# Six layer norms: the shift moves from GpSimd to VectorE

## What is computed

```python
def _ln(x, g, b):
    xf = x.astype(jnp.float32)
    mu = jnp.mean(xf, axis=-1, keepdims=True)
    var = jnp.mean(jnp.square(xf - mu), axis=-1, keepdims=True)
    return ((xf - mu) * lax.rsqrt(var + LN_EPS) * g.astype(jnp.float32) + b.astype(jnp.float32)).astype(x.dtype)

def _post(x, sub, g, b):
    return _ln(ALPHA * x + sub, g, b)
...
        yp = _post(yp, mix_p, ln_mix_g[i], ln_mix_b[i])
...
        yp = _post(yp, _cross_attn(yp, mk, mv, w_xq[i], w_xo[i]), ln_x_g[i], ln_x_b[i])
...
        yp = _post(yp, _swiglu(yp, w_gate[i], w_up[i], w_down[i]), ln_ff_g[i], ln_ff_b[i])
```

## Time and profile before

| | before |
|---|---|
| time, median of 3 runs | 3909.61 us (3906.79 to 3910.99) |
| the profiled execution: its time | 3911.87 us |
| the profiled execution: its span | 3910.1 us |
| mean granted TensorE clock | 0.942 |
| busy: PE, DVE, ACT, POOL | 3417.1, 1464.8, 1002.7, 536.6 us |
| chain that ended last: PE, DVE, ACT, POOL | 74%, 11%, 3%, 2% |

### The profile page before, as it was taken

The page is one execution under the profiler, slowest core; times in us unless marked ns, Lnnn a source line. Parts: engine busy times, 40 slices in busy tenths (PEclk is TensorE's granted clock), DMA queues, the critical chain, the costliest instruction groups (busy, mean ns, idle before and its releaser), DMA issues.

```text
span 3910.1 us, 54622 instructions
## 1 busy us (share of the span) xinstructions
PE 3417.1 (87%) x21246; PEld 3193.1 (82%) x21246; DVE 1464.8 (37%) x2121; ACT 1002.7 (26%) x1311; POOL 536.6 (14%) x331
## 2 busy tenths in 40 slices
PE   7985779799889999999599965687999799999996
PEld 6973458797889999999589954686978699999996
DVE  1555443424342212113404367755143522122125
ACT  2123442423231011012323323434232311111112
POOL 1663101200120000001300032012001300000003
PEclk9987999999999999999899988899999899999997
DMA  4673741324111111111121114322251111111111
GB/s 131 208 230 111 232 141 49 118 100 153 43 32 43 43 49 43 46 46 38 41 81 54 59 57 143 111 64 76 80 207 47 33 43 43 48 48 44 43 36 56
DMA packets 366672, 319.80 MB, mean 82 GB/s; under 512 B 19616, under 2 KB 308817, under 8 KB 366147
## 3 DMA queue, kind: packets, MB, share of 16 engines
q1 hardware_dynamic: 354783, 299.86, 24.8%
q10 hardware_dynamic: 11620, 17.77, 1.3%
q0 software_dynamic: 144, 0.52, 0.0%
HBM read 287.69 MB, written 30.74 MB: 81 GB/s over the span
## 4 chain that ended last, share of the span: by engine, by line
PE 74%; DVE 11%; DMA 5%; issue 5%; ACT 3%; POOL 2%; SPq 1%; DVEq 0%; ACTq 0%; POOLq 0%
PE ps L319 63%; PE ps L1649 2%; PE ps L1671 1%; DVE spl_w L304 1%; POOL kpage L1100 1%; PE ps L977 1%; DVE acc L2266 1%; DVE x L1444 1%; PE ps L705 1%; DMA acc<-spill_d 1%; DMA raw_w<-in_w_xv 1%; PE ps L1627 1%; DMA vpage<-in_cache_fox_v 1%; PE ps L1027 1%; ACT x L1458 1%
## 5 line engine op out<-in xcount | busy, mean ns | idle before, releaser
L319 PE MATMUL ps<-xs,spl_w 128*128 128x344 f32 x12528 | 2010.7, 323 | 55.5 <-DVE spl_w L304 27.5
L319 PEld LDWEIGHTS ps<-xs,spl_w 128*128 128x128 f32 x12528 | 2003.4, 191 | 60.1 <-DVE spl_w L304 29.5
L304 DVE TENSOR_TENSOR spl_w<-raw_w,spl_w 128x1024 fp32r<-128x1024 f32 x268 | 334.2, 1247 | 765.6 <-ACT spl_w L300 760.9
L319 PE MATMUL ps<-hs,spl_w 128*128 128x344 f32 x3168 | 513.8, 325 | 27.5 <-DVE hs L1862 27.5
L319 PEld LDWEIGHTS ps<-hs,spl_w 128*128 128x128 f32 x3168 | 512.2, 193 | 29.0 <-issue 29.0
L300 ACT CAST spl_w<-raw_w 128x1024 fp32r<-128x1024 f32 x268 | 279.5, 1043 | 393.7 <-PE ps L319 364.9
L1398 POOL MEMSET sum_x<- 128x1032 f32 x6 | 5.9, 984 | 1604.9 <-DVE hs L1862 1376.4
L1860 DVE TENSOR_TENSOR sum_x<-sq,ps 128x1032 f32<-128x1032 f32 x44 | 54.1, 1229 | 351.4 <-PE ps L319 351.4
L1406 POOL TENSOR_TENSOR sum_x<-sum_x,x 128x1032 f32<-128x1032 f32 x48 | 116.1, 2418 | 471.9 <-DVE x L1366 187.5
L1100 POOL TENSOR_TENSOR kpage<-kpage,qb 128x1024 f32<-128x1024 f32 x64 | 154.9, 2447 | 104.7 <-DMA kpage<-in_cache_fox_k 104.4
L1844 ACT CAST hs<-sum_x 128x1032 f32 (+1 forms) x44 | 46.4, 1056 | 472.2 <-DVE sum_x L1860 472.2
(11 more groups left out here) (358 smaller groups left out, 2909.0 us busy)
## 6 DMA issues: line engine op xcount, KB each, us to landing
kpage<-in_cache_fox_k SPq DMA_DIRECT2D x128, 256.0 KB, 3.2
vpage<-in_cache_fox_v SPq DMA_DIRECT2D x128, 256.0 KB, 3.0
raw_w<-in_w_gate SPq DMA_DIRECT2D x44, 512.0 KB, 3.7
raw_w<-in_w_up SPq DMA_DIRECT2D x44, 512.0 KB, 3.7
mkv<-in_cache_mem_k SPq DMA_DIRECT2D x16, 1024.0 KB, 7.9
mkv<-in_cache_mem_v SPq DMA_DIRECT2D x16, 1024.0 KB, 5.0
raw_w<-in_w_down SPq DMA_DIRECT2D x32, 512.0 KB, 3.9
raw_w<-in_w_in_cd SPq DMA_DIRECT2D x28, 512.0 KB, 3.6
```

The lines of the kernel that those rows point to most:

```text
L304: dve.tensor_tensor(spl_w[:, s, 1], raw_w[:, s], spl_w[:, s, 0].bitcast(F32), ALU.subtract).then_inc(lo_ready, 1)
L319: mm = pe.matmul(ps[:, 3 * s + t, 0:width], spl_w[:, s, a, k], part[:, k, width * t:width * (t + 1)], start=(k == 0 and step == 0), stop=( ...
```

## The change

DVE does the shift too. In the loop of norms 1, 2 and 4 it now does, per round, the product of chunk k+2, the shift of chunk k+1 and the low part of chunk k; the shift of chunk 0 stands ahead of the loop and that of chunk 7 behind it. In norms 0 and 3 each shift follows the product of the same chunk at once. In norm 5 the order per chunk is product, shift, copies. POOL's three loops of shifts are gone; its sums and everything else stay. Names, semaphores and arithmetic are the same.

```diff
--- before.py
+++ after.py
@@ -1443,11 +1443,11 @@
             xk = chunk(x, k)
             dve.tensor_tensor(xk, xk, sum_sq[:], ALU.mult).then_inc(sem("ln_scaled"), 1)
 
-        def pool_norm_shift(pool, ln, k):
-            pool.wait_ge(sem("ln_dve_step"), 2 * ln + 2)
-            pool.wait_ge(sem("ln_scaled"), DC * ln + k + 1)
+        def dve_norm_shift(dve, ln, k):
+            dve.wait_ge(sem("ln_dve_step"), 2 * ln + 2)
+            dve.wait_ge(sem("ln_scaled"), DC * ln + k + 1)
             xk = chunk(x, k)
-            pool.tensor_tensor(xk, xk, sum_x[:], ALU.add).then_inc(sem("ln_shifted"), 1)
+            dve.tensor_tensor(xk, xk, sum_x[:], ALU.add).then_inc(sem("ln_shifted"), 1)
 
         def act_norm_affine(act, ln, k):
             g = cols[:, ds(LN_G[ln] + k, 1)]
@@ -1554,6 +1554,7 @@
         def dve_memory(dve, L, ln):
             g0 = G0[f"mem{L}"]
             dve_norm_scale(dve, ln, 0)
+            dve_norm_shift(dve, ln, 0)
             for q in range(2):
                 def body(i, last=False):
                     g = g0 + 4 * q + i
@@ -1561,6 +1562,7 @@
                     split_lo(dve, 0, g + 1)
                     if not last:
                         dve_norm_scale(dve, ln, 4 * q + i + 1)
+                        dve_norm_shift(dve, ln, 4 * q + i + 1)
                     for s in range(2):
                         m = 16 * L + 8 * q + 2 * i + s
                         dve.wait_ge(sem("mem_rowsT"), m + 3)
@@ -1573,8 +1575,6 @@
                     loop(dve, 3, body)
                     body(3, last=True)
 
-        def pool_memory(pool, L, ln):
-            loop(pool, DC, lambda i: pool_norm_shift(pool, ln, i))
 
 
 
@@ -1792,19 +1792,20 @@
             act_norm_stats(act, ln)
             loop(act, DC, lambda k: act_norm_affine(act, ln, k))
 
-        def pool_norm(pool, ln):
-            loop(pool, DC, lambda k: pool_norm_shift(pool, ln, k))
 
         def dve_norm(dve, ln):
             split_lo(dve, 1, next_pair(ln))
             dve_norm_stats(dve, ln)
             dve_norm_scale(dve, ln, 0)
             dve_norm_scale(dve, ln, 1)
+            dve_norm_shift(dve, ln, 0)
 
             def body(k):
                 dve_norm_scale(dve, ln, k + 2)
+                dve_norm_shift(dve, ln, k + 1)
                 dve_norm_lo(dve, ln, k)
             loop(dve, DC - 2, body)
+            dve_norm_shift(dve, ln, DC - 1)
             dve_norm_lo(dve, ln, DC - 2)
             dve_norm_lo(dve, ln, DC - 1)
 
@@ -1891,9 +1892,12 @@
             dve_norm_stats(dve, LAST)
             dve_norm_scale(dve, LAST, 0)
             dve_norm_scale(dve, LAST, 1)
+            dve_norm_shift(dve, LAST, 0)
             for c in range(DC):
                 if c + 2 < DC:
                     dve_norm_scale(dve, LAST, c + 2)
+                if c + 1 < DC:
+                    dve_norm_shift(dve, LAST, c + 1)
                 dve.wait_ge(sem("xT_ready"), len(tiles) + c + 1)
                 if c >= 2:
                     dve.wait_ge(sem(f"rows_stored{c % 2}"), 16 * (NT // 2 + 2 * (c // 2)))
@@ -2571,12 +2575,9 @@
                     pool_states(pool)
                     pool_heads(pool)
                 pool_sums(pool, ("ab_out", "cd_out_y")[L], 3 * L)
-                pool_memory(pool, L, 3 * L)
                 pool_cross(pool, L)
                 pool_sums(pool, f"xo{L}", 3 * L + 1)
-                pool_norm(pool, 3 * L + 1)
                 pool_sums(pool, f"down{L}_2", 3 * L + 2)
-                pool_norm(pool, 3 * L + 2)
 
         @block.tensor
         def _(pe):
```

## The result

| | before | with the change |
|---|---|---|
| time, first comparison | 3908.2 us (median of 4) | 3881.15 us (3878.54 to 3882.97, 4 runs) |
| ratio, 95% interval | | 0.993 [0.9915, 0.9946] |
| ratio, two later comparisons | | 0.9937 [0.9925, 0.9949] and 0.9932 [0.9918, 0.9945] |
| the profiled execution's span | 3910.1 us | 3881.0 us |
| busy: PE, DVE, ACT, POOL | 3417.1, 1464.8, 1002.7, 536.6 us | 3412.7, 1465.8, 1002.3, 399.6 us |

A forecast was written before the change was run, and what follows sets the result against it. TensorE holds 74% of the chain; in norms 1, 2 and 4 it waits while VectorE's and GpSimd's instructions run in turn. Terms of 14.0 + 7.5 + 0.7 + 0.9 = 23.1 us gave 3888.8 or 3886.5, stated as 3888; range 3881 to 3898.

The forecast's parts named there:

- norm 1, TensorE going on: Norm 1's loop: rounds of 3.45 us instead of 4.49, TensorE's end at 35.0 instead of 42.0, 7.0 us gained.
- norm 4: Norm 4's loop, same pattern of rows as norm 1: 7.0 us gained.
- norm 2: Norm 2's tail: the next weights' load moves with the last low part, 30.10 instead of 37.59, 7.5 us gained.
- last norm: Last norm: copies keep their pace, only the start gets shorter; 0.7 us, taken between 0 and 2.0.
- norms 0 and 3, TensorE going on: Memory rounds: shifts fit into idle time, and GpSimd's stretching of a first-round low part ends; 0.9 us for both.
- The first chunk ran at the low clock: TensorE's first chunk in norms 1 and 4: about 4.8 us near 1.2 GHz; a second slow chunk would cost 1.3 us a norm.
- the 2.8 us between runs: Range's lower end, 3881: 2.8 us taken off the sum on the median for scatter between runs.
- 2.7 for handoffs: Range's lower end, 3881: a further 2.7 us taken off for handoffs shorter between some instructions.
- the memory rounds give it back: Rival, norms 0 and 3: shifts in VectorE's in-order queue hold TensorE, costing 17.5 us and the 0.9; 3906, chance 0.06.
- the slow product is VectorE's own: Rival, norms 1, 2 and 4: the loop, not GpSimd, makes the product 3.42 us; about 3970 and slower, chance 0.03.
- ScalarE did not set the pace: Rival, norms 1, 2 and 4: ScalarE's way over 4.60 us makes the pace 4.0 us; 8 us less gain, 3896, chance 0.08.
- The rule of the Trainium skill: VectorE's loop rounds: three full durations, 3.69 us; some 3.6 us less gain over three norms, about 3892.

The follow-up runs named there:

- e5: The changed kernel, with GpSimd also adding two SBUF tiles into a spare one, once per chunk in norms 1 and 4; 3909.01 us in one run.
- e4: The kernel before, with the shift moved to VectorE only in norms 0, 3 and 5; ratio 1.000 [0.9989, 1.0011].
- e7: The changed kernel plus one unused VectorE maximum, about 2.2 us, in each of the seven memory rounds with a shift; 3889.74 us in one run.

## Why the prediction came out as it did

**The mechanism was right, and the terms too.** Each of them, as forecast and as the profiles have it:

| term | forecast | measured |
|---|---|---|
| norm 1, TensorE going on (43.96 to 36.78) | 7.0 us | 7.2 us |
| norm 4 (44.0 to 36.77) | 7.0 us | 7.2 us |
| norm 2 (57.29 to 49.38) | 7.5 us | 7.9 us |
| last norm (38.31 to 37.79, 37.41, 38.10) | 0.7 us | 0.5 us (0.2 to 0.9) |
| norms 0 and 3, TensorE going on (mean 76.17 to 75.75, twice) | 0.9 us | 0.8 us |
| sum | 23.1 us | 23.6 us |

The steps inside held as well: the first low part at 7.57 (7.58), chunk 5's at 24.82 (24.74), the last at 30.10 (29.79), TensorE's end at 35.0 (34.8), the last copy at 32.5 (32.56). The last low part came 0.3 us earlier than forecast: 0.2 of it since it started 0.04 us after ScalarE's second instruction (1094.76 to 1094.80), not 0.26, and 0.1 since that instruction ended sooner. The first chunk ran at the low clock as forecast, and part of the second too. TensorE had no matmul for 13.89 us up to 1073.97; the windows from there on (PE, PEld, DVE, ACT, POOL busy, then the granted clock):

```profile
1073.90:1078.30 4.40, 4.33 (x15) 4.36 (x16) 4.40 (x4) 2.64 (x3) 0.00 (x0) 0.50 0.00 0
1078.30:1082.70 4.40, 4.40 (x26) 4.40 (x25) 4.40 (x5) 2.84 (x3) 0.00 (x0) 0.84 0.00 0
1082.70:1099.80 17.10, 17.02 (x107) 16.48 (x105) 11.89 (x11) 12.11 (x11) 0.00 (x0) 1.00 0.01 1
```

The clock of 0.50 is the 1.2 GHz level, and 0.84 a stretch in which it rose to 2.4 GHz. The chunks that were late for that were made up before chunk 5, within the slack that was forecast as 0.5 us, and cost nothing: the weight loads still waited 0.36 us for chunk 5's low part (1091.03).

**What failed is the range's lower end.** I put it at 3881, "the sum on the median less the 2.8 us between runs and less 2.7 for handoffs". The median of the first four runs is 3881.15, on that edge, and the ratio of 0.993 on 3908.2 us gives 3880.8, below it. The step that failed is the 2.8 us for the scatter between runs. I had taken it from the three runs shown, as the distance of the lowest to the median. The 36 runs of the kernel before in the three comparisons of the two kernels reach from 3900.11 to 3915.68, with a median of 3909.1, and the 15 with the change from 3878.54 to 3888.79, with a median of 3882.8. So the lowest run lies 9.0 and 4.3 us under the median, not 2.8; with 4.3 the range would have gone down to 3879.5. The medians of the three groups with the change are 3881.15, 3884.77 and 3882.8: the first is the lowest, and the other two lie inside the range. On which side of the edge the first group fell was chance. The 2.7 us for handoffs were more than enough: the terms above came out 0.5 us over the sum. And the forecast, 3888, was set above the 3886.5 that the sum on the median gives.

Where the scatter is, the table of stages shows: 677.79 to 685.42 us to the first norm in the five profiles there, and 3 to 4 us from norm 2 to 3 within each of the two kernels. In the first of these stages GpSimd waits for pages of keys, and in the five profiles this wait rises with the length of the stage, from 96.4 us (677.79) to 104.4 us (685.42). That points to the landing of DMAs, but does not show it as the cause: in e5 the wait is 98.6 us and the stage only 673.00.

**The rivals.** That the memory rounds give it back is refuted by e4 (no loss above 4 us) and by the unchanged rounds; e7 shows that of 2.3 further us a round about 1.5 would be covered. That the slow product is VectorE's own is refuted by the rows above, and e5 makes it slow again by GpSimd's reading alone. ScalarE did not set the pace: the first low part waited 0.63 us for it and started as forecast (7.58 against 7.57), and behind it the low parts of the loop never waited. The rule of the Trainium skill (VectorE: DVE Perf Modes, section The DRAIN you can't avoid) that the next VectorE instruction starts only when the last one's pipe is empty, which would have made a round 3.69 us, did not hold here: it is 3.43. The Trainium skill adds in the same section, and the prediction left out: "A next op that is not held starts earlier". The rows agree with that, 1.15 us from start to start for instructions of 1.23.

**What stays open.** The three ratios stand for 24.6, 26.6 and 27.4 us, the terms add up to 23.6. The remaining 1 to 4 us lie inside each interval. By the means of the table of stages (two profiles before, three with the change) the difference behind the first statistic is 25.1 us. The 1.5 us more than the terms lie in the stages from norm 2 to 3 and from 4 to 5 (9.3 and 7.7, where the terms at TensorE's going on are 7.9 and 7.2), which vary by about 3 us within one kernel. Whether a part of what remains is a gain of the changed program ahead of norm 0 cannot be told by these runs: the two profiles before have 683 and 685 us there, the three with the change 678 to 685, and the means differ by 3.2 us.

## What to carry to other kernels

Before GpSimd is given half of an elementwise chain beside VectorE, look whether both read two tensors from SBUF: then, as e5 shows, the two do not share the work but take turns, and the turn of GpSimd is the longer one (2.4 us against 1.2 here). One VectorE instruction more can be free if it takes away a collision; put it one step behind what it depends on, but ask which chunk the next stage waits for, the fifth or the last. And before forecasting to a tenth of a per cent, look for the stages whose length varies from run to run (here the one ahead of norm 0 and the one from norm 2 to 3): they set what can be seen.

## What was not expected of the hardware

That the turn-taking is so regular: with GpSimd reading, low parts came every 5.59 to 5.63 us, which is VectorE's 3.43 and 2.2 us more per round (5.6 - 3.4), close to the 2.4 us of a GpSimd addition alone, in both norms. And that the place of one load, behind the wait for the low parts and a few small tensors, costs more than the new loop gains in a norm: 12.1 us in norm 2 (49.38 to 37.30) against 7.9.
